# Probabilities of a chunked attention turned by VectorE and a scratch array in the first halves, with their steps spread into the next pair

## The chip, the cores and the metric

The kernel runs on one core of one Trainium2 chip. The time is the device time of one execution in microseconds (us). TensorE is PE in the rows (PEld its weight load), VectorE is DVE, ScalarE is ACT, GpSimd is POOL, SyncE is SP; a `q` behind a name is the engine's own instruction queue, where it issues transfers.

## The reference

Two layers, each over 1024 frames of width 2048, all in float32. A layer projects the frames once, and three groups of heads use the columns of that projection; their gated results go through one output projection and a layer norm.

```
h = x @ w_in                       # a_v a_gate | b_q b_k b_v b_gate | c_q c_k c_v c_gate
a_out = pool_mixer(a_v) * silu(a_gate)                   # trailing means over 2, 4, 8, 16 frames, 4 groups
b_out = swa_sink_attention(b_q, b_k, b_v) * silu(b_gate) # 16 heads of 64, window of 2 chunks, rotary, sinks
c_out = chunk_relbias_attention(c_q, c_k, c_v) * silu(c_gate)
x = layer_norm(alpha * x + concat([a_out, b_out, c_out]) @ w_out)

def chunk_relbias_attention(q, k, v, rel_bias):   # 8 heads of 64, chunks of 64 frames
    s = q @ k.T * 64**-0.5 + bias[clip(t - s)]    # own chunk and the 8 chunks before
    return softmax(s) @ v
```

The change is in the third group, called C below: between its softmax and the product with the values the probabilities have to be turned, so that the keys lie on the partitions.

## The kernel before

**Steps.** The work is cut into four steps, `it` = 0 to 3: layer 0 first half (512 frames), layer 0 second half, layer 1 first half, layer 1 second half. In a first half (`it` 0 and 2) a block of 128 queries sees only the keys of its own half: query block `j` of 0 to 3 sees `j` + 1 blocks of 128 keys. In a second half every query block sees five.

**Units.** Everything is float32, split into a high and a low part, and a product of two such matrices is three TensorE products. The weights come in units of 128 x 512 floats, each four weight tiles for PE, so a unit takes 12 matmuls of 512 columns (`quarter`, `project`). A unit is loaded by SP into a ring of four (`raw`), split by ACT into `wh` and by POOL into `wl`. A step has four pairs of C heads (`pair(p)`, 24 units each, with one group of A beside each pair), then 8 units of B keys and values, 8 tiles of B queries with 8 units each, and the output projection. Rows of the layer norm of the step before are finished in the pairs of the next (`centre`, `gain_and_bias`, `turn_rows` on DVE, loads and stores on SP).

**C in a pair.** For each query block `j` PE makes the scores of both heads into `sc` (`c_scores`), DVE adds the bias and takes the maximum (`c_max`, L1424 to L1426), ACT takes the exponential into `prob` (`c_exp`, L1026), DVE scales by the sum (`c_normalise`, L1432 and L1433), PE turns each 128 x 128 block by a product with the identity (`c_transpose`, L681), ACT and DVE split the turned blocks into the high and low part (`pt`: `c_hi`, `c_lo`), PE multiplies with the values (`c_attend`), and ACT and DVE add the parts up (`c_low_rows`, `c_add`, L1403 and L1406). These steps are written out by hand between the projection units 16 to 24 of the same pair.

**The bias rows.** In step 0, ACT's queue copies, for each pair, 128 shifted copies of the bias rows of its heads in both layers from one scratch array to another (`bias_rows`, two transfers of 384 KB on the queue that the rows call q10, L1104). SP reads them back skewed into `brope` for the pair (L521), after a wait on `tz_out`, which counts 16 for each landed transfer. All of SP's transfers stand in one list in program order (`load_unit`, L412; values stored, L420, and loaded, L427), so a wait on SP holds back each transfer behind it.

**The order on DVE** is the order of the code: copies of coefficients, the pooling sums (L1586 to L1598), the values turned (L1605), `centre` (L1527, only from step 1 on), the low part of the pooled sums (L1373), the bias rows scaled (L1619), gain and bias (L1534), low parts of keys and values and queries, then C.

Of the kernel before, what the change touches and what calls it, by code (L numbers as in the profile page):

```python
# [29 lines left out]
F32 = mybir.dt.float32  # L30
# [6 lines left out]
P = 128  # L37
# [17 lines left out]
TWOS = B_TILES // 2  # L55
C_KEYS = 640
# [22 lines left out]
O0 = B0 + B_TILES * U_B  # L79
U_STEP = O0 + 4 * U_N  # L80

# [22 lines left out]
def build(nc, x, x_t, wall, a_gw, a_scale, sinks, rel_rev, ln_gain, ln_bias, rope_cos, rope_sin,  # L104
          pool_coef, pool_inv, out):
    with ExitStack() as ctx:
# [19 lines left out]
        bval_d = nc.dram_tensor("b_values_scratch", (DEPTH, CHUNK + SEQ, P), F32, kind="Internal").ap()  # L126
        tz_d = nc.dram_tensor("bias_rows_scratch", (DEPTH * 8, P * TZ), F32, kind="Internal").ap()
# [21 lines left out]
        pt = sb("pt", [P, 5, 2, 2, P], F32R)  # L149
        pth, ptl = (pt[:, :, :, n, :] for n in range(2))  # L150
# [33 lines left out]

        ck = [m[:, MIX_B:MIX_B + 2, :].rearrange("p a n -> p (a n)") for m in (mixh, mixl)]
# [11 lines left out]
        c_low = nc.alloc_sbuf_tensor_at("c_low", [P, HALF], F32, offset=bk_at + 4 * (HD + HALF))  # L197

# [43 lines left out]
        c_out = [pv[:, 0:512], pv[:, 512:1024], pv[:, 0:512], sc[0][:, 0:512]]  # L242
        v_bank = sc[0][:, 0:512]
# [16 lines left out]
        b_pt = pt[:, :, :, :, :].rearrange("p b h l q -> p (b h l q)")[:, 0:CHUNKS * 2 * P] \  # L260
# [44 lines left out]
        hist_in = sem("hist_in")  # L305
        bias_in = sem("bias_in")
# [6 lines left out]
        ct_full = sem("ct_full")  # L313
# [63 lines left out]

        def c_seen(it, j):


            return (0, 512 - C_KEYS // 2) if half(it) else (512 - P * j, 0)

# [16 lines left out]
        def _(sp):  # L399
# [30 lines left out]
            def store_b_values(it):  # L430

                sp.wait_ge(vt_ok, (C_PAIRS + 1) * (it + 1))
                rows = bval_d[layer(it), CHUNK + half(it) * HALF:CHUNK + (half(it) + 1) * HALF, :]
                for i in range(4):
                    sp.dma_start(rows.rearrange("(j a) f -> a j f", a=32)[:, :, 32 * i:32 * (i + 1)],
                                 tmp[32 * i:32 * (i + 1), :].rearrange("a (j b) -> a j b", b=32)).then_inc(bvals_out, 16)
# [12 lines left out]

            def load_ln(it, n):  # L450

                sp.wait_ge(res_out, 64 * (it + 1) + 16)
                sp.dma_start(res[:], res_d[ds(n, 1)].rearrange("o p t n -> (o p) t n")).then_inc(ln_in, 16)
                for slot, v in enumerate((ln_gain, ln_bias)):
                    sp.dma_start(prob[:, slot, 0:512], v[layer(it), ds(n, 1), :].to_broadcast([P, 512])
                                 ).then_inc(ln_in, 16)
# [41 lines left out]
            for it in range(STEPS):  # L498
                with sp.Fori(0, C_PAIRS) as p:
                    for s in range(U_C):  # L500
                        if s == (4 if it else 0):

                            sp.wait_ge(gwl_ok, p + (C_PAIRS * it + 1))
                            sp.dma_start(gw[:], a_gw[layer(it), ds(p, 1)].rearrange("o c d -> (o c) d")
                                         ).then_inc(gw_in, 16)
                        if s == 9 and half(it):

                            sp.wait_ge(w_used, unit(it, p * U_C) + (2 + RING))
                            for m, a, b in ((mixh, 0, 3), (mixl, 3, 6)):
                                sp.dma_start(m[:, MIX_B:MIX_B + 2 * (b - a) - 1:2, :].bitcast(F32),  # L510
                                             hist_d[ds(p, 1), :, a:b, :].rearrange("o p a n -> (o p) a n")
                                             ).then_inc(hist_in, 16)
                        if s == 10:

                            sp.wait_ge(bias_ok, p + (C_PAIRS * it + 1))
                            if it:
                                sp.wait_ge(rope_ok, (B_TILES + 1) * it)
                                sp.wait_ge(bt_full, 2 * B_TILES * it)
                            else:
                                sp.wait_ge(tz_out, p * (16 * DEPTH) + 16 * DEPTH)  # L520
                            sp.dma_start(brope[:, 0, :].rearrange("p (h n) -> p h n", h=2),  # L521
                                         tz_d[ds(2 * p + 8 * layer(it), 2), 127:127 + P * (TZ - 1)]
                                         .rearrange("h (q c) -> q h c", c=TZ - 1)[:, :, 0:NEAR]).then_inc(bias_in, 16)
                        if s == 8 and it:

                            sp.wait_ge(w_used, unit(it, p * U_C) + (1 + RING))
                            load_ln(it - 1, p)
                        at = s - (15 if it else 8)
                        if at == 0:
                            store_values(it, p)  # L530
                        if at == 1:
                            load_values(it, p)
                        if s == 20 and it:
                            store_ln(it - 1, p)
                        if s in (21, 22) and turns(it):
                            store_turned(it - 1, p, s - 21)
                            if s == 22:
                                store_turned(it - 1, p, 2)
                        if s == (23 if it else 15) and not half(it):

                            wait_alone(k_ok, p + (C_PAIRS * it + 1))
                            wait_alone(v_ok, p + ((C_PAIRS + 1) * it + 1))
                            for m, a, b in ((mixh, 0, 3), (mixl, 3, 6)):
                                sp.dma_start(hist_d[ds(p, 1), :, a:b, :].rearrange("o p a n -> (o p) a n"),
                                             m[:, MIX_B + 1:MIX_B + 2 * (b - a):2, :].bitcast(F32)).then_inc(hist_out, 16)
                        if it == 0:

                            load_unit(it, p * U_C + (s + FIRST), (s + FIRST) % RING)
                        else:
                            load_unit(it, p * U_C + s, s % RING)  # L550
                        if s == 23 and it:
                            if turns(it):
                                store_turned(it - 1, p, 3)
                            wait_alone(ln_out, p * 16 + (64 * (it - 1) + 16))
                for s in range(U_KV):
                    if it or s >= FIRST:
                        load_unit(it, KV0 + s, s % RING)

                sp.wait_ge(cs_max, 8 * C_PAIRS * (it + 1))
                sp.dma_start(brope[:, 0, :], rope_cos[half(it)]).then_inc(rope_in, 16)  # L560
                sp.dma_start(brope[:, 1, :], rope_sin[half(it)]).then_inc(rope_in, 16)
                for s in range(U_B):
                    load_unit(it, B0 + s, s % RING, B0 + (s + 4) % U_B)
# [73 lines left out]
        def _(pe):  # L637
# [21 lines left out]
            def c_scores(it, p, j):  # L659
# [4 lines left out]
                for h in range(2):  # L664
                    pe.wait_ge(ct_lo, p * 8 + (8 * C_PAIRS * it + 2 * j + h + 1))
# [8 lines left out]
            def c_transpose(it, p, j):  # L674
                c0 = 0 if half(it) else 512 - P * j
                for h in range(2):

                    pe.wait_ge(cs_prob, p * 8 + (8 * C_PAIRS * it + 2 * j + h + 1))
                    for b in range(c0 // P, 5):
# [4 lines left out]
            def c_attend(it, p, j):  # L684

                if j < 3:
                    pe.wait_ge(c_fold, p * 4 + (4 * C_PAIRS * it + j + 1))

                v0 = 0 if half(it) else 4 - j
                for h in range(2):  # L690
                    pe.wait_ge(ct_lo, p * 8 + (8 * C_PAIRS * it + 2 * j + h + 1 + 2))
                    for v in range(v0, 5):
                        last = mm(c_out[j][:, 2 * P * h:2 * P * (h + 1)], cv[h][:, j + v, :],
                                  pt[:, v, h, :, :].rearrange("p l q -> p (l q)"), v == v0, v == 4)
                last.then_inc(c_pv, 1)

            def b_scores(it, v, g):

                pe.wait_ge(prod_ok, MIXES * it + 2 * C_PAIRS + 2)
# [36 lines left out]
            for it in range(STEPS):  # L736
# [7 lines left out]
                def pair(p, first=False):  # L744
# [6 lines left out]
                    else:  # L751
                        for s in range(1, 4):
                            quarter(s, 0)
# [3 lines left out]
                        for s in range(4, 8):  # L757
                            quarter(s, 1)
                    pe.wait_ge(av_ok, p + (C_PAIRS * it + 1))
# [7 lines left out]
                    if half(it):  # L767
                        pe.wait_ge(hist_in, p * 32 + (32 * C_PAIRS * layer(it) + 32))
                    c_scores(it, p, 0)
                    quarter(17, 0)  # L770
                    first = 1 + half(it)
                    quarter(18, 0, part=range(0, first))
                    c_transpose(it, p, 0)
                    quarter(18, 0, part=range(first, 4))
# [28 lines left out]
                if it == 0:  # L803
                    pair(0, True)
# [1116 lines left out]
```

## Time and profile before

| | |
|---|---|
| median of 3 runs (lowest to highest) | 2825.84 us (2825.31 to 2826.34) |
| the profiled execution | 2824.71 us |
| its span, first to last instruction | 2822.9 us |
| mean granted TensorE clock | 0.999 of full |
| busy: PE, DVE, ACT, POOL | 2807.9, 1762.0, 1297.4, 1277.3 us |
| transferred | 384.49 MB, 136 GB/s over the span |

The span is what the trace covers; the profiled execution's own time is 1.8 us longer. An idle engine other than PE costs nothing by itself. Times in the rows are counted from the start of the span.

### The profile page before, as it was taken

What the parts mean: (1) busy time and instruction counts of PE and PEld (TensorE: products, weight loads), DVE (VectorE), ACT (ScalarE), POOL (GpSimd) and SP (SyncE); (2) the same over time, 40 slices, a digit from 0 to 9 for tenths busy, and PEclk for the clock granted to TensorE, in tenths of its full rate; (3) what the DMA queues carried; (4) which work ended last, traced back from release to release, by engine and by line L of the source; (5) the groups of instructions that cost most, each with busy time, mean ns of one, the idle gap of its engine ahead of it and who ended that gap; (6) DMA issues with size and microseconds to landing.
All of it is one profiled execution on the core that took longest, in us unless ns stands there. A gap on an engine that the chain in (4) does not pass through costs nothing.

```text
span 2822.9 us, 45252 instructions
## 1 busy us (share of the span) xinstructions
PE 2807.9 (99%) x13316; PEld 2352.1 (83%) x13316; DVE 1762.0 (62%) x2950; ACT 1297.4 (46%) x2685; POOL 1277.3 (45%) x927
## 2 busy tenths in 40 slices
PE   9999999999999999999999999999999999999998
PEld 7888888888888888888888888888888888888886
DVE  5555679623777777862266666895137766678625
ACT  5444466523444445652244444664235444456521
POOL 4444444444444434444444444444444444444441
PEclk9999999999999999999999999999999999999999
DMA  6444332355555533335565663324564454333442
GB/s 212 132 133 131 100 89 82 112 175 176 169 168 167 162 91 98 86 94 179 172 192 172 174 173 105 86 82 133 155 214 133 129 155 151 100 86 84 136 157 101
DMA packets 311957, 384.49 MB, mean 136 GB/s; under 512 B 129408, under 2 KB 149920, under 8 KB 308128
## 3 DMA queue, kind: packets, MB, share of 16 engines
q1 hardware_dynamic: 308048, 367.26, 44.2%
q10 hardware_dynamic: 3792, 15.73, 1.4%
q8 instruction: 66, 1.08, 0.2%
q14 instruction: 51, 0.42, 0.0%
HBM read 327.23 MB, written 58.81 MB: 137 GB/s over the span
## 4 chain that ended last, share of the span: by engine, by line
PE 99%; DVE 0%; DMA 0%; issue 0%; ACT 0%; POOL 0%; SPq 0%; POOLq 0%
PE acc L639 70%; PE sc L639 18%; PE pv L639 9%; PE sc L681 2%; PE sc L718 1%; DMA raw<-in_wall 0%; DVE last_sums L1840 0%; DVE last_sums L1839 0%; POOL wl L1340 0%; DVE xl L1373 0%; SPq L489 0%; DVE av L1811 0%; DVE last_sums L1820 0%; ACT wh L974 0%; ACT xh L974 0%
## 5 line engine op out<-in xcount | busy, mean ns | idle before, releaser
L1340 POOL TENSOR_TENSOR wl<-raw,wh 128x512 fp32r<-128x512 f32 x920 | 1276.5, 1391 | 1501.9 <-ACT wh L974 1499.9
L974 ACT ACTIVATE wh<-raw 128x512 fp32r<-128x512 f32 x920 | 575.6, 630 | 1053.1 <-PE acc L639 722.3
L639 PE MATMUL acc<-xh,wh 128*128 128x512 f32 x2624 | 1034.0, 394 | 1.2 <-DVE xl L1373 1.2
L639 PE MATMUL acc<-xh,wl 128*128 128x512 f32 x2624 | 1022.7, 390 | 0.0
L639 PE MATMUL acc<-xl,wh 128*128 128x512 f32 x2624 | 1022.6, 390 | 0.0
L639 PEld LDWEIGHTS acc<-xh,wl 128*128 128x128 f32 x2624 | 492.6, 188 | 105.4
L639 PEld LDWEIGHTS acc<-xh,wh 128*128 128x128 f32 x2624 | 493.2, 188 | 98.2 <-DVE xl L1373 2.0
L639 PEld LDWEIGHTS acc<-xl,wh 128*128 128x128 f32 x2624 | 493.6, 188 | 94.0
L1373 DVE TENSOR_TENSOR xl<-prob,xh 128x512 f32 x48 | 55.6, 1158 | 235.8 <-ACT xh L974 235.8
L639 PE MATMUL sc<-wh,mixh 128*128 128x512 f32 x496 | 193.5, 390 | 0.1
L639 PE MATMUL sc<-wl,mixh 128*128 128x512 f32 x496 | 193.0, 389 | 0.0
L639 PE MATMUL sc<-wh,mixl 128*128 128x512 f32 x496 | 193.0, 389 | 0.0
L1373 DVE TENSOR_TENSOR pt<-sc,pt 128x512 fp32r<-128x512 f32 (+3 forms) x192 | 120.1, 663 | 80.7 <-ACT pt L974 79.7
L974 ACT ACTIVATE pt<-sc 128x512 fp32r<-128x512 f32 (+3 forms) x192 | 104.1, 577 | 82.2 <-PE sc L718 43.8
L1026 ACT ACTIVATE prob<-sc,nmax 128x640 f32<-128x640 f32 (+4 forms) x128 | 84.8, 662 | 71.9 <-DVE nmax L1426 70.0
L639 PEld LDWEIGHTS sc<-wh,mixh 128*128 128x128 f32 x496 | 93.1, 188 | 19.6 <-POOL wl L1340 0.5
L639 PEld LDWEIGHTS sc<-wh,mixl 128*128 128x128 f32 x496 | 93.1, 188 | 19.4
L639 PEld LDWEIGHTS sc<-wl,mixh 128*128 128x128 f32 x496 | 93.2, 188 | 19.1
L639 PE MATMUL acc<-wh,mixh 128*128 128x512 f32 x256 | 100.0, 391 | 0.0
L639 PE MATMUL acc<-wh,mixl 128*128 128x512 f32 x256 | 99.7, 389 | 0.0
L639 PE MATMUL acc<-wl,mixh 128*128 128x512 f32 x256 | 99.7, 389 | 0.0
L639 PE MATMUL pv<-wh,mixh 128*128 128x512 f32 x240 | 93.4, 389 | 0.0
(217 smaller groups left out, 3577.4 us busy)
## 6 DMA issues: line engine op xcount, KB each, us to landing
raw<-in_wall SPq DMA_DIRECT2D x920, 256.0 KB, 2.7
res_scratch<-res ACTq DMA_DIRECT2D x12, 1024.0 KB, 4.2
res<-res_scratch SPq DMA_DIRECT2D x12, 1024.0 KB, 4.9
res<-in_x SPq DMA_DIRECT2D x8, 1024.0 KB, 7.3
x_scratch<-res SPq DMA_DIRECT2D x8, 1024.0 KB, 5.2
x_t_scratch<-turned SPq DMA_DIRECT2D x128, 64.0 KB, 2.6
prob<-x_t_scratch SPq DMA_DIRECT2D x32, 256.0 KB, 2.8
res<-x_scratch SPq DMA_DIRECT2D x8, 1024.0 KB, 6.2
```

Source lines behind the costliest of these rows:

```text
L639: return nc.tensor.matmul(o, lhsT, rhs, start=start, stop=stop)
L681: last = nc.tensor.transpose(sc[h][:, cs], prob[:, h, cs], ident[:])
L718: last = nc.tensor.transpose(b_sc[g][:, u, c, :], probs(v, g)[:, u, c, :], ident[:])
L974: return nc.scalar.activation(o, i, ACT.Copy, scale=scale)
L1026: nc.scalar.activation(prob[:, h, c0:C_KEYS], sc[h][:, at:at + C_KEYS - c0], ACT.Exp, bias=nmax[:, h, 0:1], accum_out=psums[:, h, 0:1]).th ...
L1340: nc.gpsimd.tensor_tensor(wl[:, s, :], raw[:, s, :], wh[:, s, :].bitcast(F32), ALU.subtract).then_inc(w_lo, 1)
L1373: return V.tensor_tensor(o, whole, hi.bitcast(F32), ALU.subtract)
```

## The change

In the first halves (`it` 0 and 2) PE no longer turns the C probabilities. ACT writes the exponentials of both heads interleaved by 32 keys (`c_prob`), DVE scales them and turns all 32 x 32 blocks with one STREAM_TRANSPOSE for each query block, SP writes them in four transfers to a new array in HBM (`c_prob_scratch`) and reads them back with the keys on the partitions into `pt_raw`, from where ACT and DVE split them. Second halves keep TensorE's transposes.

As this takes longer, the steps of a query block are moved: of pair `p`, block 0 is attended at the end of the pair, and the scores of block 3 and the products of blocks 1 to 3 stand between the units of pair `p + 1` (or of the B keys behind the last pair). With them ACT's and DVE's parts move: `first_half` is DVE's new order of a pair. The pooled product (A) stays; the C product (`c_tail_product`) comes in the next pair.

Buffers that this needs move other work: SP loads gain and bias at event 13 in place of 8, the rotary tables earlier, the B query of tile 0 is projected into `sc[1]` (`q_bank`), the B values are turned into `vals` in place of `tmp`. The loops over the pairs are written out. ACT issues the bias rows of pair 1 already in pair 0, behind those of pair 0, and those of pairs 2 and 3 one pair ahead; SP's wait on `tz_out` in pair 0 is for 64 instead of 32.

```diff
+STORE_AT = (26, 29, 32, 36)
+LOAD_AT = (28, 31, 35, 38)
...
+            def store_c_prob(it, p, j):
+                n = c_kind(it, p, j)
+                if n:
+                    sp.wait_ge(cp_in, 16 * n)
+                sp.wait_ge(cs_prob, n + 1)
+                c0 = 0 if half(it) else 512 - P * j
+                keys = cprob_d[c0:C_KEYS].rearrange("(m a) r g -> r a m g", a=32)
+                for r in range(4):
+                    sp.dma_start(keys[r], both[32 * r:32 * (r + 1), 2 * c0:2 * C_KEYS].rearrange("a (m g) -> a m g", g=64)
+                                 ).then_inc(cp_out, 16)
...
+                sp.dma_start(pt_raw[:, b0:5, :], cprob_d[b0 * P:C_KEYS].rearrange("(c k) r g -> k c (r g)", k=P)
+                             ).then_inc(cp_in, 16)
...
-                                sp.wait_ge(tz_out, p * (16 * DEPTH) + 16 * DEPTH)
+                            sp.wait_ge(tz_out, max(p, 1) * (16 * DEPTH) + 16 * DEPTH)
...
 # PE, first halves, pair p
+                        quarter(1, 0)
+                        if p:
+                            c_scores(it, p - 1, 3)
+                        quarter(2, 0)
+                        quarter(3, 0)
+                        if p:
+                            c_attend(it, p - 1, 1)
...
+                        for s in range(4, 7):
                             quarter(s, 1)
+                        if p:
+                            c_attend(it, p - 1, 2)
+                        quarter(7, 1)
+                    pe.wait_ge(av_ok, p + (C_PAIRS * it + 1))
+                    for s in range(8, 11):
+                        quarter(s, 0)
+                    if p:
+                        c_attend(it, p - 1, 3)
...
+                    c_scores(it, p, 2)
+                    quarter(23, 1)
...
+                    c_attend(it, p, 0)
+                    pe.wait_ge(prod_ok, p * 2 + (MIXES * it + 3))
+                    quarter(24, 0)
...
 # ACT, pair 0 of step 0
+                    slot(8)
+                    if first:
+                        bias_rows(1)
+                    slot(9)
...
 # DVE, c_normalise
-                    V.tensor_scalar(prob[:, h, c0:C_KEYS], prob[:, h, c0:C_KEYS], rinv[:, h, 0:1], None, ALU.mult
-                                    ).then_inc(cs_prob, 1)
...
+                    rows = c_prob[:, c0 // 32:, h, :]
+                    V_(V.tensor_scalar(rows, rows, rinv[:, h, 0:1], None, ALU.mult))
+                if half(it) == 0:
+                    V.transpose(both[:, 2 * c0:2 * C_KEYS], both[:, 2 * c0:2 * C_KEYS]).then_inc(cs_prob, 1)
...
+                    coefficients(p)
+                    if p:
+                        c_normalise(it, p - 1, 3)
+                        c_add(it, p - 1, 1)
+                        c_lo(it, p - 1, 2)
+                    pooling(p)
+                    if p:
+                        c_add(it, p - 1, 2)
+                    turn_values(p)
+                    if it:
+                        centre(it - 1, p)
+                    mixed_low(p)
+                    if p:
+                        c_lo(it, p - 1, 3)
```

Two places show the order of instructions on an engine. A row is a line of the kernel's code, the operation, what it writes and reads, its shape, the number of such instructions in a row, and in brackets the semaphores that it waits for.

The first place is ACT's list in pair 0 of step 0. Before, it reads:

```order
L1104 DMA bias_rows_scratch<-bias_row_scratch 256x1x384 x2
L974 ACTIVATE wh<-raw 128x512 x2
L974 ACTIVATE av<-acc 128x512
L974 ACTIVATE bq<-gw 128x128
L974 ACTIVATE wh<-raw 128x512 x3
L974 ACTIVATE mixh<-s 128x512
L974 ACTIVATE wh<-raw 128x512 x2
```

Of the change, the same place reads:

```order
L1268 DMA bias_rows_scratch<-bias_row_scratch 256x1x384 x2
L1123 ACTIVATE wh<-raw 128x512 x2
L1123 ACTIVATE av<-acc 128x512
L1123 ACTIVATE bq<-gw 128x128
L1123 ACTIVATE wh<-raw 128x512 x2
L1268 DMA bias_rows_scratch<-bias_row_scratch 256x1x384 x2
L1123 ACTIVATE wh<-raw 128x512
L1123 ACTIVATE mixh<-s 128x512
L1123 ACTIVATE wh<-raw 128x512 x2
```

A second set of two transfers now stands some five instructions behind the first, where before the next set came only in pair 1.

The second place is DVE's list in a pair 1 to 3 of step 2, from the end of the pooling sums on (`bq<-gw,bq` is the low part of the A weights, `tmp<-acc` the values turned, `res<-res,mv,rstd` is `centre`, `mixl<-s,mixh` the low part of the pooled sums). Before:

```order
L1373 TENSOR_TENSOR bq<-gw,bq 128x128 [waits gwh_ok]
L1603 ISA [waits rel_out]
L1604 ISA [waits mixl_ok]
L1605 STREAM_TRANSPOSE tmp<-acc 128x512 [waits w_used]
L1525 ISA
L1527 TENSOR_SCALAR res<-res,mv,rstd 128x512 [waits ln_in]
L1527 TENSOR_SCALAR res<-res,mv,rstd 128x512 x3
L1356 REGISTER_ALU
L1373 TENSOR_TENSOR mixl<-s,mixh 128x512 [waits ayh_ok,dve_step]
L1616 REGISTER_ALU
L1619 TENSOR_SCALAR brope<-brope 128x256 [waits bias_in]
L1619 TENSOR_SCALAR brope<-brope 128x256
```

Of the change:

```order
L1646 TENSOR_TENSOR bq<-gw,bq 128x128 [waits gwh_ok]
L1676 TENSOR_TENSOR c_low<-pv,c_low 64x512 [waits c_low_ok]
L1679 TENSOR_TENSOR c_att<-c_low 64x128 [waits dve_step]
L1679 TENSOR_TENSOR c_att<-c_low 64x128
L1900 STREAM_TRANSPOSE tmp<-acc 128x512 [waits w_used,mixl_ok,rel_out]
L1813 TENSOR_SCALAR res<-res,mv,rstd 128x512 [waits ln_in]
L1813 TENSOR_SCALAR res<-res,mv,rstd 128x512 x3
L1646 TENSOR_TENSOR mixl<-s,mixh 128x512 [waits ayh_ok,dve_step]
L1646 TENSOR_TENSOR pt<-pt_raw,pt 128x4x256 [waits ct_hi]
L1906 TENSOR_SCALAR brope<-brope 128x256 [waits bias_in]
L1906 TENSOR_SCALAR brope<-brope 128x256
```

The sum of block 2 of the pair before (`c_add`, three instructions) now stands ahead of the turned values, and the low part of its block 3 (`pt<-pt_raw,pt`, which PE's product of block 3 needs) stands behind `centre` and the low part of the pooled sums.

## Rows read from the trace of the kernel before

**Rows 1.** Page: busy line, and engine shares of the chain that ended last.

```profile
PE 2807.9 (99%) x13316; PEld 2352.1 (83%) x13316; DVE 1762.0 (62%) x2950; ACT 1297.4 (46%) x2685; POOL 1277.3 (45%) x927
...
PE 99%; DVE 0%; DMA 0%; issue 0%; ACT 0%; POOL 0%; SPq 0%; POOLq 0%
```

**Rows 2.** Waits of PE: us in total, times, longest us.

```profile
PE sc L735 <- POOL ident L1333: 1.6, 1, 1.6
PE acc L639 <- DVE xl L1373: 1.2, 2, 0.9
```

**Rows 3.** Groups of PE, forms apart: busy us, mean ns of one, idle before.

```profile
L681 PE MATMUL sc<-ident,prob 128*128 128x128 f32 x480 | 63.3, 273 | 0.0
...
L735 PE MATMUL sc<-ident 128*128 128x128 f32 x20 | 4.5, 424 | 1.6 <-POOL ident L1333 1.6
```

**Rows 4.** Timeline of PE, 57 to 82 us: start us, us, instruction.

```profile
57.20 0.39 PE L639 MATMUL acc<-xh,wh 128*128 128x512 f32 x1
...
58.33 0.39 PE L639 MATMUL acc<-xh,wl 128*128 128x512 f32 x1
58.56 0.38 PE L681 MATMUL sc<-ident,prob 128*128 128x128 f32 x2
...
59.01 0.39 PE L639 MATMUL acc<-xl,wh 128*128 128x512 f32 x1
...
79.64 0.39 PE L639 MATMUL acc<-xh,wl 128*128 128x512 f32 x1
79.87 1.11 PE L681 MATMUL sc<-ident,prob 128*128 128x128 f32 x8
...
81.05 0.39 PE L639 MATMUL acc<-xl,wh 128*128 128x512 f32 x1
```

**Rows 5.** DMA in 24:34 (40 slices, queue), 34:44, 44:48: packets, MB, share.

```profile
GB/s 215 129 127 272 270 133 74 92 84 49 45 55 49 49 49 55 49 49 49 49 49 49 156 145 106 156 236 320 164 156 49 213 309 377 109 51 47 131 320 424
...
q10 hardware_dynamic: 267, 0.41, 11.0%
...
q10 hardware_dynamic: 248, 0.38, 10.0%
...
q1 hardware_dynamic: 773, 0.50, 40.2%
```

**Rows 6.** Timelines of ACT, SP, DVE and PE, 20 to 55 us.

```profile
22.38 3.89 ACTq L1104 DMA_DIRECT2D bias_rows_scratch<-bias_row_scratch  x2
...
46.66 0.38 SPq L521 DMA_DIRECT2D brope<-bias_rows_scratch  x1
...
51.30 0.62 DVE L1619 TENSOR_SCALAR brope<-brope 128x256 f32<-128x256 f32 x2 [5.10 <-DMA brope<-bias_rows_scratch]
...
51.97 0.63 ACT L974 ACTIVATE wh<-raw 128x512 fp32r<-128x512 f32 x1 [2.53 <-DMA raw<-in_wall]
...
54.37 0.33 PE L639 MATMUL sc<-mixh 128*128 128x128 f32 x2
```

**Rows 7.** Last window: us, busy of each engine, granted clock, DMA share, GB/s.

```profile
2815.00:2823.00 8.00, 0.00 (x0) 0.00 (x0) 4.93 (x7) 0.00 (x0) 0.00 (x0) 0.53 0.35 131
```

**Rows 8.** Timeline of DVE in pair 1 of step 2.

```profile
1495.10 1.57 DVE L1586 TENSOR_TENSOR s<-av 128x527 f32<-128x527 f32 x1 [3.58 <-ACT av L974]
...
1502.13 0.28 DVE L1373 TENSOR_TENSOR bq<-gw,bq 128x128 fp32r<-128x128 f32 x1
1504.69 0.72 DVE L1605 STREAM_TRANSPOSE tmp<-acc 128x512 f32<-128x512 f32 x1 [2.27 <-PE acc L639]
1505.33 3.01 DVE L1527 TENSOR_SCALAR res<-res,mv,rstd 128x512 f32<-128x512 f32 x4
1508.67 1.38 DVE L1373 TENSOR_TENSOR mixl<-s,mixh 128x512 fp32r<-128x512 f32 x1 [0.32 <-ACT mixh L974]
...
1545.93 0.68 DVE L1403 TENSOR_TENSOR c_low<-pv,c_low 64x512 f32<-64x512 f32 x1
1546.64 1.68 DVE L1406 TENSOR_TENSOR c_att<-c_low 64x128 f32<-64x128 f32 x2
```

**Rows 9.** Page, DMA issues: count, KB each, median us to landing.

```profile
gate<-values_scratch SPq DMA_DIRECT2D x16, 256.0 KB, 3.3
```

More of the change, by code:

```diff
@@ L79 @@
 O0 = B0 + B_TILES * U_B
+O0_BEGIN = B0 + U_B
 U_STEP = O0 + 4 * U_N
@@ L453, in load_ln, with load_gain_bias @@
                 sp.dma_start(res[:], res_d[ds(n, 1)].rearrange("o p t n -> (o p) t n")).then_inc(ln_in, 16)
+            def load_gain_bias(it, n):
+                if n and not half(it + 1):
+                    sp.wait_ge(cp_out, 64 * c_kind(it + 1, n, 0))
                 for slot, v in enumerate((ln_gain, ln_bias)):
@@ L1170, in pair @@
                     mix_hi(p * 2 + (nb + 2), p + MIX_C)
-                    if not half(it):
-                        act.wait_ge(hist_out, p * 32 + (32 * C_PAIRS * layer(it) + 32))
-                if it == 0:
-                    pair(0, True)
-                with act.Fori(int(it == 0), C_PAIRS) as p:
-                    pair(p)
-                for s in range(2, 5):
-                    split(it, KV0 + s, s % RING)
-                split(it, KV0 + 5, 1)
-                act.wait_ge(rope_ok, (B_TILES + 1) * it + 1)
@@ L1194, in _, with query_hi, b_keys_hi @@
-                split(it, B0 + 4, 0)
+                for p in range(C_PAIRS):
+                    if half(it):
+                        second_half(p)
+                    else:
+                        pair(p, it + p == 0)
+                last = C_PAIRS - 1
+                def query_hi():
+                    act.wait_ge(rope_ok, (B_TILES + 1) * it + 1)
+                    b_queries_hi(0, s0[:, 0:HALF]).then_inc(qh_ok, 1)
+                def b_keys_hi():
+                    if half(it):
+                        act.wait_ge(hist_mv, layer(it) + 1)
+                    act.wait_ge(rope_ok, (B_TILES + 1) * it + 2)
+                    keys_hi([k[:, HD:] for k in bk], s0[:, 0:HALF]).then_inc(qh_ok, 1)
@@ L1634, in _, with second_half @@
+                def second_half(p):
+                    coefficients(p)
+                    pooling(p)
+                    turn_values(p)
+                    centre(it - 1, p)
+                    mixed_low(p)
+                    bias_rows_ready(p)
+                    gain()
+                    bias()
+                    low_keys(p)
+                    if turns(it):
+                        turn_rows(it - 1, p)
+                    low_values(p)
                     queries_lo(cq, acc[1], SCALE, p * 2 + 2 * pc)
```

598 lines of the change are left out of this document (431 added, 167 removed).

## The prediction

> **What bounds the kernel now.** I read the page first. PE is busy for 2807.9 of 2822.9 us, and the chain that ended last is PE to 99% [rows 1]. Then the waits of PE: 1.6 us for the identity at the start and 1.2 us for an early low part, 2.8 us in all [rows 2]. The kernel is one unbroken stream of matmuls, so a column taken off PE is a gain, a wait put into the stream is a loss, and nothing else counts. The profiled execution took 2824.71 us, 1.1 us under the median of 2825.84. I sum against 2824.7; the difference is below what a measurement of this kernel can tell, which I take as 0.2%, or 5.65 us.
>
> **What leaves PE.** The turning is L681, 480 matmuls, 63.3 us by busy time [rows 3]. Busy time overstates it, since each matmul is drawn with its latency. What it costs is the delay of the next product. In the stretch without turning, five products start between 57.20 and 58.33, one each 0.226 us [rows 4]. A block of 2 turnings stands behind the product of 58.33, and the product of 59.01 is the second behind it; without the block the two would be two pitches apart, so it costs 0.68 - 0.45 = 0.23 us. A block of 8 costs 1.41 - 0.45 = 0.96 us in the same way (79.64 to 81.05) [rows 4]. Between them lie about 0.12 us a turning, so the 2 + 4 + 6 + 8 of a pair of a first half cost 0.23 + 0.45 + 0.67 + 0.96 = 2.3 us. Eight such pairs: **18.4 us** leave PE. That is the whole gain that is to be had, 0.65%. Scores, products and projection units are the same in number. The products now read the turned blocks in runs of 32 elements instead of whole rows; no row shows such an operand. From below the cost is nothing, from above it is a doubling: 20 products of 256 columns a pair at 0.113 us, 2.3 us a pair or 18 us in all, which would eat the gain. Nearest is the product with whole rows, as the number of columns is the same, so I take 0 and keep the other end for the rivals.
>
> **Pair 0 of step 0: a wait on SP.** This is the largest counter-term. The set of bias rows of pair 0 is issued on ACT's queue at 22.38 [rows 6]. The queue's packets are 267 in 24 to 34 us, 248 in 34 to 44, and none in 44 to 48 [rows 5]: the set takes about 20 us, 0.79 MB. In the slices in which nothing else moves the rate is 49 GB/s, against over 300 where weights move [rows 5]; at 49 GB/s alone 0.79 MB take 16 us. So one set saturates what little of the DMA engines it uses, and its time is not a latency. SP reads the rows back at 46.66, just after the set is through, DVE gets them at 51.30, ACT's next weight at 51.97 stands behind that same SP transfer, and PE starts the scores at 54.37 with no wait [rows 6].
>
> In the changed kernel a second, equal set stands on the same queue some five ACT instructions behind the first, and SP's wait in pair 0 is for both. The second set can start when the first leaves its engines and takes 16 us (alone) to 20 us (as the first did): it ends at 60 to 64 us. SP stands at that transfer from 46.7 on, with the next five weight units behind it, so the chain of [rows 6] moves as a whole: 46.66 becomes 60 to 64, 54.37 becomes 68 to 71, and PE stops for 13 to 17 us. While SP stands, no new weights move, so the second set runs nearer to its time alone: I take its end at 61.3, less a slack of 0.4 that I guess from DVE and ACT following each other without a pause there. **+14.2**.
>
> The Trainium skill ("DMA: Bandwidth & Descriptors", section "Why a DMA increments its semaphore by 16 and not by 1") says that a hardware-queue transfer uses the largest number of engines up to 16 that divides the slowest dimension on both sides, and always the lowest-numbered ones. For two heads that would be two engines, the same two for either set. The 49 GB/s in the idle slices agrees with that [rows 5]; by this rule the sets follow each other, and the sum is as above, where transfers free to use other engines would give rival D.
>
> PE's clock may fall in such a stop: in the last 8 us, without a matmul, the granted clock is 0.53, nearer 1.2 than 2.4 GHz [rows 7]. The price of coming back is bounded from below by 0 and from above by the opening turnings of the program: 20 in 4.5 us at 424 ns each, where 273 ns is the mean of L681 [rows 3] and 0.12 us the marginal cost, so 4.5 - 2.4 = 2.1 us, with the ends 2.3. PE comes from a standstill in both, so I take **+2.3**.
>
> **DVE in step 2.** The steps of query blocks 1 to 3 move into the next pair, and PE's product of block 3 stands behind unit 10. Counted from the start of unit 1, it is due after ten units of 12 products (27.1 us), the scores of block 3 (four products, 0.9) and the products of blocks 1 and 2 (4 and 6 of half size, 1.1): at **29.2 us**.
>
> What it needs is the low part of block 3, which DVE makes behind a chain. The turned block 2 can only be read back into `pt_raw` when PE is through with block 1, at 9.5 us. A transfer of such a kind lands 3.3 us after its issue [rows 9], here about 13.3. ACT's high part takes some 0.9 and DVE's low part about 1.2: 15.4. Then, in DVE's new order, the pooling, 7.3 us from 1495.10 to the end of 1502.41 [rows 8]: 22.7. The sum of block 2: 0.68 and 0.6 to 1.68 [rows 8], take 1.6: 24.3. The values turned, 0.72: 25.0. `centre`, 3.01: 28.0. The low part of the pooled sums, 1.38 [rows 8]: 29.4. The low part of block 3, 1024 elements, where 512 take 1.38: 1.4 to 2.8, take 1.9: 31.3. That is 2.1 us after it is due, with 1 to 3.5 from the bounds. PE stops for that in the pairs 1 to 3 of step 2: **+6** (3 to 10). In step 0 there is no `centre`, the chain ends at 28.3, and PE hides it by 0.9 us. Behind the last pair of a step the units of B keys stand, where DVE has neither pooling nor `centre`.
>
> **What else moves.** STREAM_TRANSPOSE on DVE adds for each query block about what the values' turning takes (0.72 for 512 columns, [rows 8]), so up to 1.4, and PE no longer waits behind it, as these blocks are read a pair later. ACT's high parts are as many. The scores' exponentials wait for the store of the block before (`cp_out`); the stores are issued two to four units ahead, 5 to 11 us. SP has five transfers more for each block, 20 in a pair; in step 2 they compete with the stores of the layer norm. I put down **+1** for a late A product there (0 to 4). Both second halves keep their order. DMA has room: 136 GB/s now, 21 MB more in 384.
>
> **The sum.** 2824.7 - 18.4 + 14.2 + 2.3 + 6 + 1 = 2829.8, so **2830 us**, 0.15% over the median: no change that can be told.
>
> **The rivals.** *A, the forecast* (chance 0.50): gain, wait in pair 0 and late DVE, 2824 to 2836 us. *B, DVE is in time in step 2* (0.20): the chain above is short by 2 us of guesses (the low part of 1024 elements, the landing), and only pair 0 stops: 2824.7 - 18.4 + 16.5 = 2823, up to 2826. *C, SP is crowded in step 2* (0.12), slower: its list also holds the layer norm's loads and stores and the four stores of each turned block, and the turned block 2 is read back behind them. Each us by which it lands after 13.3 stops PE one us more, in three pairs. Landing twice as late after its issue (7 us, as two transfers in a row would take) gives 3.5 more a pair, 2830 + 10.5 = 2840. It decides from 0.6 us a pair on, which brings the sum over 2831.5. For it speaks the number of transfers, against it that a load of such a kind takes 3.3 us in the median now [rows 9]. *D, the sets run beside each other* (0.08): the second set uses other DMA engines, both land at about 49 us, SP is late by some 3 to 5 us and the clock holds: 2815 to 2820, faster. Against it speaks the low rate, the same for 20 us with two transfers in flight [rows 5]. *E, all hidden* (0.06): the rows land earlier, or the wait is taken up by weights already in the ring, and DVE is in time: 2824.7 - 18.4 = 2806 to 2808. Against it: the next weight stands behind that transfer on SP, and four units in the ring are 11 us. *F, the strided operand is paid for* (0.04): 2.3 us a pair, 2830 + 18 = 2848.
>
> **How the numbers follow.** Slower by over 0.2% means above 2831.5, faster below 2820.2. A reaches from 2824 to 2836 and lies above 2831.5 in some four of ten cases (0.20 slower, 0.30 same), by the spread of the bounds of its wait and of the DVE chain. B is the same, but for a small part below (0.16 same, 0.04 faster). C and F are slower (0.16). D and E are faster (0.14). That gives 0.18 faster, 0.46 same, 0.36 slower. The range of 8 in 10 goes from 2814 (D within) to 2841 (C within) and leaves out E and F; A's own is 2824 to 2836.
>
> **What would show it.** L681 falls from 480 to 320 instructions. PE's waits list scores behind `q_ok` or a weight behind `raw` at about 55 to 70 us, 13 to 17 us once, with DVE's bias row line at about 65 to 68 instead of 51.3; the queue q10 works without a gap from 24 to over 60. The granted clock shows less than 1.0 right behind it. In step 2 there are three waits of 1 to 3.5 us of `pv` products for DVE's low part. Wrong would be: q10 at double rate with both sets in flight (D), or PE with no wait longer than 1 us in pair 0 (E); products with the turned blocks at more than 0.113 us from start to start would be F.

## The result

The changed kernel takes 2840.17 us in the median of five runs (2837.61 to 2843.26), the kernel before 2825.84 (2825.01 to 2826.34): a ratio of 1.0053, 95% interval 1.0038 to 1.0067. It is slower by half a per cent. The forecast was 2830 with a range of 2814 to 2841, no change as the likeliest outcome and 0.36 for slower: the time lies just inside the range, the likeliest outcome did not come.

The profiled execution is the slowest of the five, 2843.26 us with a span of 2841.5, so it lies 3.1 us over the median. Its page answers to [rows 1]:

```profile
PE 2803.1 (99%) x13156; PEld 2343.0 (82%) x13156; DVE 1802.0 (63%) x2950; ACT 1274.9 (45%) x2644; POOL 1281.5 (45%) x927
...
PE 92%; DVE 3%; DMA 2%; issue 1%; SPq 1%; ACT 0%; ACTq 0%; POOL 0%; POOLq 0%; DVEq 0%
```

PE has 160 instructions less, and is still named 99% busy: busy time hides what happened, as a matmul at a lower clock counts as more of it. The chain tells more. PE was 99% of the chain before and is 92% now; the rest are waits for DVE, DMA and the issuing queues. The waits of PE (us in total, times, longest; against 2.8 us in [rows 2]):

```profile
PE acc L710 <- POOL wl L1613: 12.2, 3, 7.3
PE sc L710 <- DVE mixh L1658: 5.3, 1, 5.3
PE pv L710 <- DVE pt L1646: 3.9, 3, 1.8
PE acc L710 <- DVE xl L1646: 3.0, 4, 1.3
PE sc L815 <- POOL ident L1606: 1.6, 1, 1.6
```

Where the time went is read by comparing when the same projection unit starts in both timelines of PE. Unit 12 of a pair is a good place for it, as all C work of the pair before is done by then in either kernel. The "shift" is how much later the unit starts in the changed kernel:

```
place (first matmul of the unit)     before     after    shift   (us)
step 0, pair 0, unit 12               40.77     50.19    +9.42
step 0, pair 1, unit 12              114.49    132.24   +17.75
step 0, pair 3, unit 12              261.22    275.35   +14.13
step 0, unit 20 of the B tiles       381.96    398.65   +16.69
step 2, pair 0, unit 12             1442.02   1458.67   +16.65
step 2, pair 3, unit 12             1662.11   1679.27   +17.16
step 2, unit 20 of the B tiles      1782.86   1802.01   +19.15
last product of PE                  2810.58   2829.57   +18.99
```

A pair whose turning has left PE would shift it by -2.3 us; what a stretch lost is its shift with these 2.3 us added back. So pair 0 of step 0 lost 20.0 us (9.42 + 8.33 + 2.3, of which 2.0 before 23 us, at the start of the program), the two stretches behind the last pairs lost 4.9 and 4.3, the way from pair 0 to pair 3 of step 2 lost 7.4, and the way from pair 1 to pair 3 of step 0 lost 1.0. The second halves shift by nothing (from the last row of step 0 to the first of step 2: 16.69 to 16.65).

**Pair 0.** ACT's and SP's queues and PE, in the timeline:

```profile
24.98 3.89 ACTq L1268 DMA_DIRECT2D bias_rows_scratch<-bias_row_scratch  x2
...
32.16 15.80 ACTq L1268 DMA_DIRECT2D bias_rows_scratch<-bias_row_scratch  x2
48.06 0.63 ACT L1123 ACTIVATE wh<-raw 128x512 fp32r<-128x512 f32 x1 [15.29 <-issue]
...
65.85 0.37 SPq L584 DMA_DIRECT2D brope<-bias_rows_scratch  x1
...
68.67 0.62 DVE L1906 TENSOR_SCALAR brope<-brope 128x256 f32<-128x256 f32 x2 [13.30 <-DMA brope<-bias_rows_scratch]
...
50.19 0.76 PE L710 MATMUL acc<-xh,wh 128*128 128x512 f32 x1 [7.27 <-POOL wl L1613]
...
71.33 0.69 PE L710 MATMUL sc<-mixh 128*128 128x128 f32 x2 [5.34 <-DVE mixh L1658]
```

There are two stops, not one. ACT itself stood for 15.8 us in the issue of the second set, with the weight splits behind it: that is the first stop, 42.9 to 50.2. Then SP stood at the same transfer as forecast, to 65.85 (the forecast said 61.3; [rows 6] has 46.66), and the second stop came at 66.0 to 71.3. The queue q10 in 24 to 44 us, 44 to 48 (where [rows 5] has none) and 48 to 66 (packets, MB, share of the time of 16 engines):

```profile
q10 hardware_dynamic: 442, 0.68, 9.0%
...
q10 hardware_dynamic: 115, 0.17, 11.5%
...
q10 hardware_dynamic: 475, 0.72, 10.7%
```

Together these are 1032 packets, twice the 515 of [rows 5], at no higher rate: the second set followed the first. In the windows of the stops and behind them the granted clock is the third number from the end, ahead of the DMA share and the GB/s:

```profile
42.50:50.20 7.70, 0.43 (x3) 0.04 (x1) 0.96 (x1) 2.14 (x5) 1.43 (x2) 0.82 0.14 47
50.20:54.00 3.80, 3.80 (x9) 3.03 (x10) 1.78 (x4) 2.94 (x6) 3.48 (x3) 0.50 0.55 163
...
65.50:71.30 5.80, 0.49 (x3) 0.07 (x1) 2.09 (x7) 1.91 (x4) 1.26 (x1) 1.00 0.72 214
71.30:78.00 6.70, 6.63 (x17) 5.29 (x18) 1.88 (x5) 1.14 (x2) 2.55 (x2) 0.50 0.89 291
```

Behind either stop PE ran at 1.2 GHz, 0.43 us from product to product in place of 0.23, which cost 1.9 and 3.0 us more.

**Behind the last pair.** ACT's timeline in step 0, and PE (`mixh<-tmp` is the high part of the C product):

```profile
347.74 2.54 ACT L1123 ACTIVATE b_keys<-s 64x512 fp32r<-64x512 f32 x4
357.80 0.63 ACT L1123 ACTIVATE mixh<-tmp 128x512 fp32r<-128x512 f32 x1 [7.51 <-DVE tmp L1686]
358.34 1.13 ACT L1123 ACTIVATE wh<-raw 128x512 fp32r<-128x512 f32 x2
...
360.44 0.47 PE L710 MATMUL acc<-xh,wh 128*128 128x512 f32 x1 [2.45 <-POOL wl L1613]
```

ACT waits 7.5 us for the C product that now comes late, and two weight splits stand behind it. PE loses 2.6 us, and again 1.5 behind it, eight products at about 0.43 us from start to start; the same follows at 1761 us in step 2. The forecast had named this stretch as free.

### The profile page after: what moved, and what is told of

It reads as the page before. It is cut to its first block, busy times and chain, and to the rows that moved or that the text cites. A ratio compares the mean times of both kernels' runs of the same rounds, so it can differ in the third digit from the quotient of the medians.

```text
span 2841.5 us, 41322 instructions
## 1 busy us (share of the span) xinstructions
PE 2803.1 (99%) x13156; PEld 2343.0 (82%) x13156; DVE 1802.0 (63%) x2950; ACT 1274.9 (45%) x2644; POOL 1281.5 (45%) x927
## 4 chain that ended last, share of the span: by engine, by line
PE 92%; DVE 3%; DMA 2%; issue 1%; SPq 1%; ACT 0%; ACTq 0%; POOL 0%; POOLq 0%; DVEq 0%
PE acc L710 63%; PE sc L710 18%; PE pv L710 9%; PE sc L754 1%; PE sc L798 1%; DMA bias_rows_scratch<-bias_row_scratch 1%; DMA raw<-in_wall 0%; DMA c_prob_scratch<-prob 0%; SPq L533 0%; DVE pt L1646 0%; DVE mixl L1646 0%; ACTq L1268 0%; DVE s L1882 0%; DVE res L1813 0%; DVE s L1880 0%
## 5 line engine op out<-in xcount | busy, mean ns | idle before, releaser
L710 PE MATMUL acc<-xh,wh 128*128 128x512 f32 x2560 | 1011.1, 395 | 15.4 <-POOL wl L1613 12.2
L710 PE MATMUL acc<-xh,wl 128*128 128x512 f32 x2560 | 1001.1, 391 | 0.0
L710 PE MATMUL acc<-xl,wh 128*128 128x512 f32 x2560 | 1001.0, 391 | 0.0
L710 PEld LDWEIGHTS acc<-xh,wh 128*128 128x128 f32 x2560 | 483.5, 189 | 112.8 <-issue 15.5
L710 PEld LDWEIGHTS acc<-xh,wl 128*128 128x128 f32 x2560 | 482.6, 189 | 103.7
L710 PEld LDWEIGHTS acc<-xl,wh 128*128 128x128 f32 x2560 | 483.8, 189 | 92.4
L1646 DVE TENSOR_TENSOR pt<-sc,pt 128x512 fp32r<-128x512 f32 (+1 forms) x128 | 91.5, 751 | 51.6 <-ACT pt L1123 51.1
L1123 ACT ACTIVATE pt<-sc 128x512 fp32r<-128x512 f32 (+1 forms) x128 | 79.5, 647 | 67.6 <-PE sc L798 43.7
L710 PE MATMUL pv<-wl,mixh 128*128 128x512 f32 x240 | 93.4, 389 | 0.0
```

The costliest lines, as they stand in the source:

```text
L710: return nc.tensor.matmul(o, lhsT, rhs, start=start, stop=stop)
L1123: return nc.scalar.activation(o, i, ACT.Copy, scale=scale)
L1646: return V.tensor_tensor(o, whole, hi.bitcast(F32), ALU.subtract)
```

## The experiments

Theory 1: one set of bias rows goes through few DMA engines, a second set behind it holds up ACT's issue and SP's wait; the stretches behind the last pairs (the tails) and DVE's list in step 2 are separate losses. The rivals are in the expectations. A ratio is against the kernel before, measured beside the run.

**rows_spread.** The two outer dimensions of the transfers of a set change places:

```diff
-act.dma_start(tz_d[heads].rearrange("h (q c) -> h q c", c=TZ),
-              rel_d[heads].rearrange("h (o c) -> h o c", o=1).to_broadcast([2, P, TZ])
+act.dma_start(tz_d[heads].rearrange("h (q c) -> q h c", c=TZ),
+              rel_d[heads].rearrange("h (o c) -> o h c", o=1).to_broadcast([P, 2, TZ])
```

> The changed kernel with the dimensions of the two transfers of a bias-row set exchanged, so that the 128 shifts and not the 2 heads are outermost; bytes, order and waits stay. Theory 1 (a set goes through two DMA engines, and the second set queues behind the first, which holds up both ACT, whose issue of it took 15.8 us, and SP's wait): ACT issues it in about 4 us, q10 is through before 45 us, no stop of PE in pair 0, which cost about 20 us; 2840 - 18 to 20 = 2820 to 2823 us. Theory 2 (HBM or the scratch array is the limit, not the engines): unchanged, 2838 to 2843. Theory 3 (the stop is SP's alone, ACT's long issue is harmless): also 2820 to 2823; the next run tells 3 from 1.

2823.1 us (2821.4 to 2824.32), ratio 0.9988, interval 0.9979 to 0.9997. Its ACT queue:

```profile
23.85 1.30 ACTq L1268 DMA_DIRECT2D bias_rows_scratch<-bias_row_scratch  x2
...
30.74 1.21 ACTq L1268 DMA_DIRECT2D bias_rows_scratch<-bias_row_scratch  x2
```

Its queue q10 in 24 to 34 and in 34 to 44 us (packets, MB, share):

```profile
q10 hardware_dynamic: 777, 1.13, 40.1%
...
q10 hardware_dynamic: 311, 0.44, 18.1%
```

Both sets, twice the bytes of [rows 5], are through before 44 us (a transfer lands 5.1 us after its issue in the median); neither ACT nor SP stands, and 17 us come back. Bytes, order and waits are those of the changed kernel, so theory 2 (HBM) falls. From the shares one can work out what changed: 40.1% of the time of 16 engines is 6.4 engines at work, where the 11.5% of the changed kernel are 1.8. A packet took 83 ns (40.1% of 16 engines in 10 us, for 777 packets), and 64 ns in the changed kernel, so more engines, and not faster packets, made the difference. That the order of the dimensions decides is what the Trainium skill says ("DMA: Bandwidth & Descriptors", section "Why a DMA increments its semaphore by 16 and not by 1": the slowest dimensions give the number of engines); the run agrees.

**rows_own_count.** SP waits for the first set alone:

```diff
-sp.wait_ge(tz_out, max(p, 1) * (16 * DEPTH) + 16 * DEPTH)
+sp.wait_ge(tz_out if p else tz_first, max(p, 1) * (16 * DEPTH))
...
-).then_inc(tz_out, 16)
+).then_inc(tz_out if q else tz_first, 16)
```

> The changed kernel with a semaphore of its own for the first set, so that SP in pair 0 waits for the first set alone; the second set is still issued at the same place and still slow. Theory 1: ACT still stands some 16 us in the issue of the second set, PE still stops 7 to 8 us at 42 us with half clock behind it (together about 10), the second stop of 5.5 us and its slow clock (together about 8 to 9) is gone: 2831 to 2833. Theory 3 (SP's wait alone): both stops gone, 2820 to 2823.

2832.31 us (2831.67 to 2833.89). ACT's issue of the second set still takes 16.27 us, PE's first stop is 7.7 us, and the second is gone. So ACT's stand in the issue is a loss of its own, and mending the wait alone brings back only half (7.9 us of 17): theory 3 falls.

**before_second_set.** The other direction: the kernel before, with a set into a spare array that nobody reads, and SP's wait in pair 0 for it.

```diff
+spare_d = nc.dram_tensor("spare_rows_scratch", (DEPTH * 8, P * TZ), F32, kind="Internal").ap()
...
 slot(8)
+if first:
+    for head in range(0, DEPTH * 8, 8):
+        heads = ds(2 + head, 2)
+        act.dma_start(spare_d[heads].rearrange("h (q c) -> h q c", c=TZ),
+                      rel_d[heads].rearrange("h (o c) -> h o c", o=1).to_broadcast([2, P, TZ])
+                      ).then_inc(spare_out, 16)
...
+sp.wait_ge(spare_out, 16 * DEPTH)
```

> The kernel before, with one more set of bias rows issued at the same place of pair 0, into a spare array that nobody reads, and SP's wait in pair 0 also for it. Theory 1: the whole loss of pair 0 without any of the rest of the change: 2826 + 17 to 21 = 2843 to 2847, with the same two stops. If the stop needs the other edits (their transfers, the new order), less than 5 us: 2826 to 2831.

2843.2 us (2841.58 to 2843.89), ratio 1.0059, interval 1.0046 to 1.0073. Its waits of PE:

```profile
PE acc L642 <- POOL wl L1349: 6.6, 1, 6.6
PE sc L642 <- DVE mixh L1394: 6.3, 1, 6.3
```

The same two stops without any other part of the change: the second set costs 17 us by itself.

**tail_only.** The changed kernel with two moves in ACT's list behind the last pair:

```diff
+b_keys_hi()
 split(it, B0 + 4, 0)
-b_keys_hi()
-mix_hi(nb + 2 * C_PAIRS, last + MIX_C)
...
 split(it, B0 + 7, 3)
+if half(it) == 0:
+    mix_hi(nb + 2 * C_PAIRS, last + MIX_C)
```

> The changed kernel, where behind the last pair of a first half ACT makes the high parts of the B keys before one weight split and the high part of the C product behind the last weight split of tile 0 in place of ahead of two of them. Theory 1 (PE's stops at 357 and 1761 us, 4.3 us each with the slow clock, come from weight splits that stand behind ACT's wait for the C product): both gone, 2840 - 8.5 = 2831 to 2832. Rival (the stop moves to the scores of the first B tile, as DVE's rotation is late whatever ACT does): 2838 to 2841.

2833.64 us (2833.1 to 2836.27), 6.5 less than the changed kernel, 2 short of what was expected. In step 2 the stop is gone; in step 0 a wait of 1.5 us is left, for DVE's turned B values: there DVE's four low parts of the B keys took 4.85 us, against 3.78 in step 2. The kernels below that have this edit (all_mended and those named spread_tail) also make DVE's sum of block 3 ahead of those keys, and no stop is left there.

**before_spread**, the control: the dimensions changed as in rows_spread, in the kernel before.

> Control: the kernel before with the exchanged dimensions of the bias-row transfers and nothing else. By all theories the transfers are hidden there: 2825 to 2827 us, the same. If it is faster by over 2 us, that part of what rows_spread gained is not due to the change.

2824.78 us (2824.35 to 2827.77), ratio 0.9996, interval 0.9987 to 1.0005: the same. Where the transfers are hidden their engines do not matter.

**dve_spread.** rows_spread with two moves in DVE's list of a first-half pair:

```diff
 if p:
-    c_max(it, p - 1, 3)
     c_lo(it, p - 1, 1)
+    c_max(it, p - 1, 3)
...
 turn_values(p)
+if p:
+    c_lo(it, p - 1, 3)
 if it:
     centre(it - 1, p)
 mixed_low(p)
-if p:
-    c_lo(it, p - 1, 3)
```

> rows_spread (2823.1 us) with two moves in DVE's order of a first-half pair: the low part of block 1 ahead of the maximum of block 3, and the low part of block 3 ahead of the centring and of the low part of the pooled sums. Theory (PE's stops in step 2, together 3 to 5 us in rows_spread, come from DVE's low parts that stand behind other work in DVE's list): 2818.5 to 2820.5. Rival (they come from the turned blocks landing late, which DVE's order does not change, or the moves make the score of block 0 late instead): 2822 to 2825.

2827.49 us (2825.67 to 2828.78): 4.4 slower than rows_spread, where 2.6 to 4.6 faster was expected. The waits for `pt` are down to 0.2 us as meant, but new ones came:

```profile
PE acc L710 <- DVE mixl L1646: 4.4, 3, 1.5
PE sc L710 <- DVE mixh L1658: 2.9, 3, 1.0
```

DVE's timeline in pair 2 of step 2, with a line of ACT's, has the reason:

```profile
1577.76 0.72 DVE L1900 STREAM_TRANSPOSE tmp<-acc 128x512 f32<-128x512 f32 x1
1581.09 1.23 DVE L1646 TENSOR_TENSOR pt<-pt_raw,pt 128x1024 fp32r<-128x1024 f32 x1 [2.62 <-ACT pt L1123]
1582.23 3.85 DVE L1813 TENSOR_SCALAR res<-res,mv,rstd 128x512 f32<-128x512 f32 x4
...
1580.00 1.06 ACT L1123 ACTIVATE pt<-pt_raw 128x1024 fp32r<-128x1024 f32 x1 [1.96 <-DMA pt_raw<-c_prob_scratch]
```

Moved ahead of the centring, the low part of block 3 makes DVE stand for ACT for 2.6 us, and ACT itself stands for the read-back of the turned block. The whole list behind it, to the keys and queries of the next scores, is late by that. The centring had filled this gap; both halves of the rival were right.

**all_mended.** dve_spread with the mended tails.

> dve_spread with the edit of tail_only as well, and with DVE's sum of block 3 of the last pair ahead of its low parts of the B keys. If the three losses add up (pair 0, the tails, DVE in step 2), what is left is the gain of 18.4 us less about 2 to 3 us of small waits and of start: 2819.5 - 8 to 9 = 2810 to 2812. If a loss only moves to the next wait: 2814 or more.

2818.8 us (2818.0 to 2820.89), ratio 0.9974, interval 0.9963 to 0.9986. That is 7 us over what was expected, because the sum started from a time for dve_spread that did not come. Against the measured dve_spread the tails bring 8.7 us, so they add up; DVE's moves still cost.

**spread_tail**, and once more as **spread_tail_again**: rows_spread and the mended tails, DVE's order in the pairs that of the changed kernel.

> all_mended with DVE's order of the changed kernel put back: exchanged dimensions of the bias-row transfers and the mended tails alone. Theory (the three losses are separate places, and the moves in DVE's list cost 4 us): rows_spread's 2823.1 - 8.5 = 2814 to 2815.5. If the tails' gain depended on the moved list: 2818 or more.

> spread_tail once more beside it on the same chip, as its five runs lay 4 us apart: 2813 to 2817 us by the theory that the start of the program (2 to 3 us, before the first unit) is what varies.

2815.11 us (2812.54 to 2816.73), ratio 0.9959, interval 0.9946 to 0.9973; and again 2813.89 (2812.89 to 2814.7), ratio 0.9958, interval 0.9944 to 0.9971. Both are as expected, and beat both kernels: 0.4% faster than before. Its waits of PE, the second time:

```profile
PE acc L710 <- DVE xl L1647: 2.4, 4, 1.6
PE sc L815 <- POOL ident L1607: 1.6, 1, 1.6
PE pv L710 <- DVE pt L1647: 1.0, 1, 1.0
PE sc L710 <- DVE mixl L1659: 0.9, 3, 0.3
```

**spread_tail_dve2** moves less: the low part of block 3 stays behind the centring, but ahead of `mixed_low`; the low part of block 1 ahead of the maximum.

```diff
 if it:
     centre(it - 1, p)
-mixed_low(p)
 if p:
     c_lo(it, p - 1, 3)
+mixed_low(p)
```

> spread_tail with a smaller move: DVE's low part of block 3 behind the centring, as in the changed kernel, but ahead of the low part of the pooled sums (0.7 us), and the low part of block 1 ahead of the maximum of block 3. Theory (in step 2 DVE has no idle time left in the first 35 us of a pair, so only an order that never stands helps): DVE does not wait for ACT in front of the low part of block 3, 1 to 3 us less than spread_tail, 2812 to 2814. Rival (each move there only shifts the stop to the keys and queries behind): 2815 to 2819.

2819.48 us (2816.86 to 2822.72), some 5 slower than spread_tail: the rival was right, the stop moved to the queries. PE no longer waits for `pt`, but 4.3 us in three stops for the queries (`mixh` L1659).

**spread_tail_turn** then puts the turning of the normalised rows behind the queries:

```diff
-if turns(it):
-    turn_rows(it - 1, p)
 low_values(p)
 queries_lo(cq, acc[1], SCALE, p * 2 + 2 * pc)
+if turns(it):
+    turn_rows(it - 1, p)
```

> spread_tail_dve2 with the four transposes of the normalised rows (2.5 us, DVE) behind the low parts of the C values and queries, which PE's scores of block 0 wait for, in place of ahead of them. Theory (DVE's list of step 2 has no slack up to the queries; what moves the stop is the order alone, and the rows have slack behind the queries): the three stops of 1.5 us at the scores of block 0 and their slow start vanish, 2819.5 - 4 to 6 = 2813.5 to 2815.5, about as spread_tail or 1 us better. Rival (the rows then reach the scratch array late, ACT stands in its wait for them, and the A product and the weight splits behind it come late): 2819 or more.

2827.97 us (2825.23 to 2830.97): 8 slower than spread_tail_dve2, not 4 to 6 faster. A wait of ACT in spread_tail_dve2 and here, then the timelines of SP, ACT and PE in pair 2 of step 2:

```profile
ACT wh L1123 <- DMA raw<-in_wall: 28.6, 12, 4.8
...
ACT wh L1123 <- DMA raw<-in_wall: 60.5, 17, 5.2
...
1594.91 0.33 SPq L449 DMA_DIRECT2D raw<-in_wall  x1
1601.14 1.98 SPq L533 DMA_DIRECT2D x_t_scratch<-turned  x4
...
1617.02 0.63 ACT L1123 ACTIVATE wh<-raw 128x512 fp32r<-128x512 f32 x1 [4.40 <-DMA raw<-in_wall]
1617.55 0.58 ACT L1147 ACTIVATE gate<-acc 128x512 f32<-128x512 f32 x1
...
1618.91 0.68 PE L710 MATMUL acc<-mixh,bq 128*128 128x512 f32 x1 [2.42 <-DVE gate L1666]
```

SP stood for the late rows with the next weights behind them in its list, ACT then split late, with the gate behind the split, and PE waited 8.2 us in four stops at the A product for a gate. The rival had the direction right; that SP's weights, not ACT's own wait, would carry the delay was in neither.

## Why the prediction was right or wrong

The range held, and the point lay 10 us low. The gain and the wait in pair 0 had the right mechanism, step 2 only in part, and one loss was not seen at all. That the range held is in part luck: its upper end, 2841, stood for rival C, and 2840 came about by other terms; the forecast's own range ended at 2836. By its terms, against the shifts of the profiled execution:

```
term                                   forecast   measured
turning off PE                           -18.4      -18.4   (taken with 2.3 a pair, see below)
pair 0: stops                            +14.2      +12.9   (7.4 + 5.5)
pair 0: slow clock behind them            +2.3       +4.9   (1.9 + 3.0)
step 2: DVE late, SP                      +7         +7.4
behind the last pairs of steps 0 and 2     0         +9.2   (4.9 + 4.3)
small waits in step 0                      0         +1.0
start of the program                       0         +2.0
```

The right column adds up to 19.0 for the last product of this execution; between the medians lie 14.3.

**The gain** was right. In dve_spread, where nothing stops between unit 12 of pairs 0 and 1 of step 2, the shift goes from -1.76 to -4.08: 2.32 us a pair. The strided operand costs nothing that counts: in step 0 two products with turned blocks start 0.120 us apart in the mean, 0.118 before. Rival F falls.

**Pair 0** was right in cause and nearly in size, and wrong in its way. The forecast let ACT issue the second set in passing and put the whole loss on SP's wait. rows_own_count shows that ACT's issue stops PE by itself. The two losses overlap in time, since the first stop delays what SP's wait holds up, so their sum is near the one forecast: when the second stop ends, PE is 17.0 us late, 2.0 of them from the start of the program, and the 15.0 left stand against 14.2. Rival D falls with q10's packets, as the sets did follow each other; E falls with the two stops.

**The slow clock** was priced for one stop, and there were two, each with its own slow stretch. Behind the second, which is the one forecast, it cost 3.0 us for 2.3. That this came near is partly luck: the price was read from the opening turnings, where the granted clock reads 1.00 (1.6 to 6.4 us), so no row tied it to a slow clock. The 1.9 behind the first lie inside the 15.0 just named, as SP's transfer at 65.85 sets the end of the second stop; that it would end there without the first stop too was not tried.

**Step 2** came out at 7.4 us for a forecast of 7, but not as the chain had it, three stops of about 2 us at block 3; that the sizes agree is luck. The largest was 1.8 us at block 1 of pair 1, which is attended in pair 2, and two of about 1 at block 3 followed, 3.9 us in all; behind the largest the granted clock fell to 0.54 for 3.7 us, and the rest are small waits. The trace shows where the largest came from:

```profile
ACT prob L1184 <- DMA c_prob_scratch<-prob: 26.7, 12, 4.1
...
1569.61 0.58 ACT L1184 ACTIVATE prob<-sc,nmax 128x384 f32<-128x384 f32 x1 [2.97 <-DMA c_prob_scratch<-prob]
...
1571.40 0.69 DVE L1646 TENSOR_TENSOR mixl<-tmp,mixh 128x512 fp32r<-128x512 f32 x1 [3.83 <-ACT mixh L1123]
...
1578.98 0.68 DVE L1646 TENSOR_TENSOR pt<-pt_raw,pt 128x512 fp32r<-128x512 f32 x1
...
1579.80 0.57 PE L710 MATMUL pv<-pt,mixh 128*128 128x256 f32 x2 [1.83 <-DVE pt L1646]
```

ACT's exponential waits for the store of the block before, ACT's high part of the A product stands behind it, DVE waits for that part, and its list then runs without a gap to the low part that PE needs. The prediction had named this wait for the store and put it at nothing, with the store issued 5 to 11 us ahead; here it was issued at 1564.43, and ACT was ready for the exponential at 1566.6. No run changed this. The three kernels that reorder work there show what the forecast's chain did not say: DVE's list in this stretch has no slack, and each edit of the order moved the stop and made it dearer. Rival B falls with the stops. SP crowded, rival C, did not come as its mechanism: the read-backs landed 2.8 to 4.6 us after their issue in the median, not 7. Its time, 2840, did come, by other terms.

**The step that failed** is the sentence that behind the last pair "the units of B keys stand, where DVE has neither pooling nor `centre`", and with it a price of nothing. True of DVE, it left out ACT: there the high part of the C product stands ahead of weight splits, and waits for a product that DVE now makes only behind the low parts of the B keys, the sum of block 3 and the rotation of the first B query. tail_only shows the cause, and with the sum moved as well the whole stop is gone in both steps. It cost 9.2 us; with them the forecast would have read 2839. A second step failed in pair 0, without much effect on the sum: the issue of the second set, put at nothing for ACT, took it 15.8 us.

What stays open: why the start of the program, before the first C work, takes 0.6 to 3.9 us longer in the changed kernels (the shift of unit 12 of pair 0 is +0.57 in rows_spread, +3.86 and +1.30 in the two profiles of spread_tail), and what the small waits of 0.5 us a pair in step 0 are made of; neither was tried.

## What to carry to other kernels

A transfer that was hidden need not be cheap: look at how many DMA engines it uses, by its rate when nothing else moves, before a second one is put behind it, and count the issuing engine's own time as a wait. When work moves across a loop's edge, follow each of its parts on every in-order list in the last round as well as in the middle, and ask what stands behind the instruction that will now wait, weight splits above all. On an engine with no idle time left, moving an instruction ahead to mend one wait can open a gap that something else had filled.

## What the runs showed of the hardware

Two transfers in flight, whose rows of 1.5 KB are laid out with 2 heads outermost, moved at 49 GB/s together when nothing else did; the same bytes with 128 shifts outermost landed 5.1 us after the issue in the median, where a set had taken 20. Issuing two such transfers took 3.9 us of ACT's queue the first time, 15.8 us when two more were still under way, and 1.2 to 2.4 us in the kernels with the dimensions exchanged. A stop of PE of 5.3 us, in a window in which the granted clock still reads 1.00, was followed by 6.7 us at 0.50; one of 7.3 us by 3.8 us at 0.50; one of 1.8 us in step 2 by 3.7 us at 0.54.
